# One transformer step on one core: attention with row-half scores, and token-major matmuls of 512 columns

## The chip, the cores and the metric

One core of a Trainium2 chip runs the whole program. The core has TensorE (PE, matmul), VectorE (DVE), ScalarE (ACT), GpSimd (POOL) and SyncE (SP, which here only issues DMAs). TensorE's weight loads have a row of their own in the profile (PEld). Time is device microseconds of one execution; the figure given for a kernel is the median of its runs.

## What is computed

One layer of a diffusion backbone on 640 tokens of width 1024: four tiles of 128 latent tokens and one tile of 128 context tokens. The weight matrices are in float32. Cut to what matters here:

```python
h = rmsnorm(x, norm1_g) * (1.0 + scale1) + shift1          # adaLN, scale and shift from c @ w_ada
q_r, k_r, v_r, g_r, q_d, k_d, v_d, gates = split(h @ w_in)
branch_r = (silu(g_r) * group_norm(retention(q_r, k_r, v_r))) @ w_ret_out
# differential attention, 8 heads, two maps of width 64 in each head:
s = einsum('bqhmd,bkhmd->bhmqk', q_d, k_all) * 64 ** -0.5  # latent queries: 512 latent + 128 cached keys
p = softmax(s, axis=-1)                                    # context queries: 128 context keys
o = einsum('bhqk,bkhe->bqhe', p[:, :, 0] - lam * p[:, :, 1], v_all)
branch_d = (rmsnorm(o, subln_g) * 0.8) @ w_diff_out
x = x + gate1 * ((gate_r * branch_r + gate_d * branch_d) @ w_o)
h2 = rmsnorm(x, norm2_g) * (1.0 + scale2) + shift2
x = x + gate2 * ((silu(h2 @ w_ffn_gate) * (h2 @ w_ffn_up)) @ w_ffn_down)
y = rmsnorm(x, final_norm_g)
```

## The kernel before

Every engine has its own instruction stream, written out by hand, and the streams meet only at semaphores (`wait_ge`, `then_inc`). So the order on each engine is the order in the code.

**Dense phases.** `PHASES` lists 17 of them, in units of 256 columns of a weight matrix. The weights of a unit are a slot of 8 k-tiles x 256 columns; there are two slots. SP streams a unit into `w_raw`, ScalarE rounds it to float32r (`w_hi`, `act_split`), VectorE takes the rest (`w_lo`, `dve_split`), and each product is three matmuls: low x high, high x low, high x high, with the activations split in the same way. Two kinds of unit exist. `pe_T_unit` (line 330) holds weights stationary and streams 320 tokens; its result is feature-major. `pe_N_unit` (line 347) holds 128 tokens stationary and streams 256 weight columns; its result is token-major. The phases v_r, g_r, v_d, w_o, down0, down1 and down2 use the second kind: for each unit, for each of 5 token tiles, for each k, three matmuls. Units of even and odd `par` use PSUM banks 0 to 3 and 4 to 7; `mm_done` is raised after tile 3 and after tile 4 of a unit. The reader takes the four latent tiles in one instruction and the context tile in another (`copy_N` on ScalarE, `residual` on VectorE; `block_sums` then squares on ScalarE). With `split` a phase begins before its input is whole: at the first tile of the first unit TensorE waits at each k.

**Attention.** It works through 8 heads x 5 query tiles, n = 5h + t; tiles 0 to 3 are latent (640 keys), tile 4 is context (128 keys). A tile's stages: GpSimd copies a query tile into `qz`, once for each of two maps, with the other 64 rows at zero; TensorE computes `scores` for a map over all 128 rows (512 + 128 keys) into banks 0 and 1, or 2 and 3; VectorE takes the `maximum`; ScalarE the `exp` with its row sum; VectorE in `weights` the reciprocals, the factor of the second map, and p0 + factor x p1 over all keys; TensorE transposes the result (`weights_T`, banks 4 and 5); ScalarE evacuates it (`evacuate_T`); TensorE multiplies by the values (`outputs`, bank 6 or 7); ScalarE evacuates, in a square with its sum and a scaled copy (`evacuate_o`). The scores of a tile are issued one step ahead of its weights and three ahead of its outputs; the loop runs over heads, the five tiles of a step are written out. All of attention's matmuls are in float32, which the profile shows as two passes each.

After the last transposes GpSimd makes eight products (`diag`, line 635) that TensorE needs to spread the gates over rows.

Of the kernel before, what the change touches and what calls it, by code (L numbers as in the profile page):

```python
# [30 lines left out]
ACT = mybir.ActivationFunctionType  # L31
# [15 lines left out]
DH = 8  # L47
# [20 lines left out]

def lay_out_phases():
# [6 lines left out]
    for name, n, *readers in PHASES:  # L76
        first[name], count[name], reader[name] = unit, n, readers
        before[name] = list(last)
        start[name] = dict(total)
        same = readers[0] == readers[1]  # L80
        for s in range(2):
# [13 lines left out]
PBUF = (0, 1, 2, 0, 1)  # L95
TBUF = (0, 1, 0, 1, 2)
# [20 lines left out]
def tile_of(h, t):  # L117

    return h + t // TILES, t % TILES, h * TILES + t


def build(nc, a, o):

    with ExitStack() as ctx:
# [21 lines left out]
        qz = at("qz", H + 35, [P, TILES, 2, P])  # L146
# [45 lines left out]
        gated = at("gated", M + 10, [P, 4, UC])  # L192
# [26 lines left out]
        sm = small("sm", [P, TILES, 7])  # L219
# [8 lines left out]
        def bank(b, n=BANK, at_=0):  # L228
            return psum[:, b * BANK + at_:b * BANK + at_ + n]

# [11 lines left out]


# [22 lines left out]
        ada_step = sem("ada_step")  # L266

# [16 lines left out]
        at_z, at_qz, at_s, at_max, at_e = sem("at_z"), sem("at_qz"), sem("at_s"), sem("at_max"), sem("at_e")  # L284

        at_r, at_f, at_a, at_T, at_aT, at_o = (sem(n) for n in ("at_r", "at_f", "at_a", "at_T", "at_aT", "at_o"))
        at_oe = sem("at_oe")
# [59 lines left out]
        def pe_N_unit(pe, name, i, par, hi, lo, kt=KT, split=None):  # L347

            for t in range(TILES):
                ts = slice(t * P, (t + 1) * P)  # L350
                for k in range(kt):
                    if split and par == 0 and t == 0:
                        pe.wait_ge(split[0], split[1] + k + 1)
                    for n, (w, x) in enumerate(((w_lo[par], hi), (w_hi[par], lo), (w_hi[par], hi))):
                        last = pe.matmul(bank(4 * par + t // 2, UC, (t % 2) * UC), x[:, k, ts], w[:, k, :],  # L355
                                         start=(k == 0 and n == 0), stop=(k == kt - 1 and n == 2))
                if name in ADA_FIRST and t == LAT_TILES:
                    last = pe_ada_sums(pe, name, i, par)
                if t >= LAT_TILES - 1:
                    last.then_inc(mm_done, 1)  # L360
# [108 lines left out]
        def _(sp):  # L469
# [29 lines left out]

            by_tile = {n: a[n][0].rearrange("(k p) c -> p k c", p=P)  # L500
                       for n in ("w_ret_out", "w_diff_out", "w_o", "w_ffn_gate", "w_ffn_up", "w_ffn_down")}
            stream("v_r", columns(w_in, 1024))
            stream("g_r", columns(w_in, 2048))
# [5 lines left out]
            stream("v_d", columns(w_in, 5120))  # L509
            stream("diff_out", columns(by_tile["w_diff_out"], 0))  # L510
            stream("w_o", columns(by_tile["w_o"], 0))
            for third in range(3):
                c0, kt = third * D, min(KT, FFN // P - third * KT)
                stream(f"up{third}", [(by_tile["w_ffn_gate"], c0, UC, KT), (by_tile["w_ffn_up"], c0, UC, KT)])
                stream(f"down{third}", columns(by_tile["w_ffn_down"][:, third * KT:third * KT + kt, :], 0, kt))
# [11 lines left out]
        def _(pool):  # L527
# [85 lines left out]
            pool.memset(qz[:, :, :, :], 0.0).then_inc(at_z, 1)  # L613
            pool.wait_ge(at_z, 1)

            def fill_qz(t, src):
                for m in range(2):
                    r = slice(m * DHD, (m + 1) * DHD)
                    pool.tensor_copy(qz[r, t, m, :], src(r)).then_inc(at_qz, 1)

            for t in range(TILES):
                fill_qz(t, lambda r: qk_d[r, 0, t * P:(t + 1) * P])
            pool.wait_ge(at_oe, 2)
            pool.dma_start(o["new_diff_k"][0, 0].rearrange("p h m d -> p (h m d)"), k_out[:, :]).then_inc(k_stored, 16)
            with pool.Fori(1, DH) as h:
                for t in range(TILES):
                    pool.wait_ge(at_s, h * (2 * TILES) + (2 * t + 2 - 2 * TILES))
                    fill_qz(t, lambda r: qk_d[r, bass.ds(h, 1), t * P:(t + 1) * P])


            pool.wait_ge(at_T, DH * TILES)
# [12 lines left out]
        def _(pe):  # L644
# [36 lines left out]
            pe_dense(pe, "v_r", pe_N_unit, h_hi, h_lo)  # L681
            pe_dense(pe, "g_r", pe_N_unit, h_hi, h_lo)
# [59 lines left out]
            pe_dense(pe, "v_d", pe_N_unit, h_hi, h_lo)  # L742
# [10 lines left out]
            def scores(h0, t0, m, first=False):  # L753
                h, t, n = tile_of(h0, t0)
                pe.wait_ge(at_qz, n * 2 + (m + 1))
                if not first:
                    pe.wait_ge(at_e, n * 2 + (m - 1))
                if t < LAT_TILES:
                    k = qk_d[:, bass.ds(h + DH, 1), 0:LAT].rearrange("p a i -> p (a i)")
                    pe.matmul(bank(2 * m), qz[:, t, m, :], k, start=True, stop=True)  # L760
                    k = kc_T[:, bass.ds(h, 1), :].rearrange("p a i -> p (a i)")
                    last = pe.matmul(bank(2 * m + 1, P), qz[:, t, m, :], k, start=True, stop=True)  # L762
                else:
                    k = qk_d[:, bass.ds(h + DH, 1), LAT:TOK].rearrange("p a i -> p (a i)")
# [745 lines left out]
```

## Time and profile before

| what | value |
|---|---|
| median of 3 runs | 1433.07 us (1432.6 to 1435.84) |
| profiled execution, span | 1432.7 us |
| TensorE busy | 1363.0 us, 95% |
| weight loads busy | 1291.3 us, 90% |
| VectorE busy | 638.5 us, 45% |
| ScalarE busy | 452.0 us, 32% |
| GpSimd busy | 112.9 us, 8% |
| mean granted TensorE clock | 0.988 of full |

Busy is the time in which at least one instruction of the engine was under way. Matmuls overlap, so 95% does not say that the array works for 95% of the time; how far apart matmuls start says more. Waits of an engine matter where they lie on the chain that ends last.

### The profile page before, as it was taken

To read this page: it belongs to the slowest core of one execution; us is meant where nothing else is said; L and a number is where in the kernel's file an instruction comes from. 1 tells how busy PE (TensorE), PEld (TensorE's weight loads), DVE (VectorE), ACT (ScalarE), POOL (GpSimd) and SP (SyncE) were. 2 spreads that over 40 slices of the span, in tenths; PEclk is the share of its full clock that TensorE was granted. 3 is DMA by queue.
4 is the path that set the end of the run, shared out by engine and by line. 5 is a ranking of instruction groups with operands and counts; after the bars stand their busy time and mean duration, and the time that the engine had idled before them with its cause. 6 is when DMAs were issued, how large, how long until landed. Compare 5 with 4: busy or idle time off the path is not lost.

```text
span 1432.7 us, 24335 instructions
## 1 busy us (share of the span) xinstructions
PE 1363.0 (95%) x9545; PEld 1291.3 (90%) x9545; DVE 638.5 (45%) x935; ACT 452.0 (32%) x777; POOL 112.9 (8%) x205
## 2 busy tenths in 40 slices
PE   4899999999999999998999899989999999999996
PEld 1699998899999999996777599989999999999996
DVE  3733112466557534645777644352324232333244
ACT  5421313344211122216777522242211122212223
POOL 1011000300111111202111300000000000000000
PEclk9999999999999999999999999999999999999998
DMA  9444231143444343530000014202121212221211
GB/s 303 146 116 118 59 88 44 53 134 116 144 150 137 103 128 101 168 128 30 0 0 0 30 59 147 89 30 88 59 88 61 87 59 88 73 75 61 72 45 73
DMA packets 100820, 127.05 MB, mean 89 GB/s; under 512 B 3433, under 2 KB 91986, under 8 KB 100770
## 3 DMA queue, kind: packets, MB, share of 16 engines
q1 hardware_dynamic: 90624, 95.20, 21.1%
q0 software_dynamic: 8928, 30.09, 6.7%
q10 hardware_dynamic: 1218, 1.07, 0.2%
q8 instruction: 34, 0.56, 0.2%
q14 instruction: 16, 0.13, 0.0%
HBM read 115.34 MB, written 4.72 MB: 84 GB/s over the span
## 4 chain that ended last, share of the span: by engine, by line
PE 88%; DVE 4%; issue 2%; SPq 2%; ACT 2%; POOL 1%; DMA 1%; DVEq 0%; ACTq 0%; POOLq 0%
PE psum L340 49%; PE psum L355 26%; PE psum L760 4%; PE psum L787 2%; PE psum L774 2%; SPq L481 1%; PE psum L321 1%; DVE probs L1359 1%; PE psum L762 1%; PE psum L671 1%; DMA ada_a<-in_w_ada 1%; POOL diag L635 1%; PE psum L388 1%; PE psum L389 1%; PE psum L722 1%
## 5 line engine op out<-in xcount | busy, mean ns | idle before, releaser
L305 DVE TENSOR_TENSOR w_lo<-w_raw,w_hi 128x2048 fp32r<-128x2048 f32 x78 | 178.7, 2291 | 307.8 <-ACT w_hi L300 299.8
L340 PE MATMUL psum<-h_hi,w_lo 128*128 128x320 f32 x1344 | 308.5, 311 | 3.4 <-DVE hf L431 1.4
L340 PE MATMUL psum<-h_hi,w_hi 128*128 128x320 f32 x1344 | 307.4, 310 | 0.0
L340 PE MATMUL psum<-h_lo,w_hi 128*128 128x320 f32 x1344 | 307.2, 310 | 0.0
L340 PEld LDWEIGHTS psum<-h_hi,w_lo 128*128 128x128 f32 x1344 | 225.4, 189 | 4.4 <-issue 4.3
L340 PEld LDWEIGHTS psum<-h_lo,w_hi 128*128 128x128 f32 x1344 | 225.9, 189 | 0.0
L340 PEld LDWEIGHTS psum<-h_hi,w_hi 128*128 128x128 f32 x1344 | 225.7, 189 | 0.0
L300 ACT ACTIVATE w_hi<-w_raw 128x2048 fp32r<-128x2048 f32 x77 | 146.8, 1906 | 149.1 <-PE psum L355 97.7
L355 PE MATMUL psum<-w_lo,h_hi 128*128 128x256 f32 x480 | 136.1, 283 | 0.0
L355 PE MATMUL psum<-w_hi,h_lo 128*128 128x256 f32 x480 | 135.8, 283 | 0.0
L355 PE MATMUL psum<-w_hi,h_hi 128*128 128x256 f32 x480 | 135.8, 283 | 0.0
L355 PE MATMUL psum<-w_lo,hid_hi 128*128 128x256 f32 x440 | 124.9, 284 | 1.7 <-DVE hid_lo L1453 1.7
L355 PE MATMUL psum<-w_hi,hid_lo 128*128 128x256 f32 x440 | 124.5, 283 | 0.0
L355 PE MATMUL psum<-w_hi,hid_hi 128*128 128x256 f32 x440 | 124.5, 283 | 0.0
L355 PEld LDWEIGHTS psum<-w_hi,h_lo 128*128 128x128 f32 x480 | 92.1, 192 | 0.0
L355 PEld LDWEIGHTS psum<-w_hi,h_hi 128*128 128x128 f32 x480 | 92.1, 192 | 0.0
L355 PEld LDWEIGHTS psum<-w_lo,h_hi 128*128 128x128 f32 x480 | 92.1, 192 | 0.0
L1140 DVE SCALAR_TENSOR_TENSOR ada_acc<-ada_b,silu_c,ada_acc 128x256 f32<-128x256 f32 x224 | 90.0, 477 | 0.0
L355 PEld LDWEIGHTS psum<-w_lo,hid_hi 128*128 128x128 f32 x440 | 84.4, 192 | 2.6 <-DVE hid_lo L1453 2.6
L355 PEld LDWEIGHTS psum<-w_hi,hid_hi 128*128 128x128 f32 x440 | 84.5, 192 | 0.0
L355 PEld LDWEIGHTS psum<-w_hi,hid_lo 128*128 128x128 f32 x440 | 84.4, 192 | 0.0
L1343 DVE TENSOR_REDUCE sm<-psum 128x1 f32<-128x640 f32 (+1 forms) x80 | 57.4, 717 | 42.5 <-PE psum L762 38.8
(214 smaller groups left out, 1842.6 us busy)
## 6 DMA issues: line engine op xcount, KB each, us to landing
w_raw<-in_w_in SPq DMA_DIRECT2D x32, 1024.0 KB, 5.9
ada_b<-in_w_ada POOLq DMA_DIRECT2D x32, 512.0 KB, 4.1
w_raw<-in_w_ffn_gate SPq DMA_DIRECT2D x11, 1024.0 KB, 5.1
w_raw<-in_w_ffn_up SPq DMA_DIRECT2D x11, 1024.0 KB, 5.1
ada_a<-in_w_ada SPq DMA_DIRECT2D x8, 1024.0 KB, 12.4
w_raw<-in_w_ffn_down SPq DMA_DIRECT2D x8, 1024.0 KB, 5.1
w_raw<-in_w_ret_out SPq DMA_DIRECT2D x4, 1024.0 KB, 5.1
swapped<-qk_d POOLq DMA_DIRECT2D x32, 128.0 KB, 2.5
```

What stands on the lines that cost most here:

```text
L300: act.activation(w_hi[s][:, :, :], w_raw[s][:, :, :], ACT.Copy).then_inc(w_hi_done, 1)
L305: dve.tensor_tensor(w_lo[s][:, :, :], w_raw[s][:, :, :], w_hi[s][:, :, :].bitcast(F32), ALU.subtract).then_inc(w_lo_done, 1)
L321: last = pe.matmul(out[:, 2 * m + c:2 * m + c + 1], ada_acc[:, slot, c, m * P:(m + 1) * P], ones_col[:, :], start=True, stop=True)
L340: last = pe.matmul(bank(4 * par + 2 * j + h, HALF), w[:, k, cs], x[:, k, h * HALF:(h + 1) * HALF], start=(k == 0 and n == 0), stop=(k == K ...
L355: last = pe.matmul(bank(4 * par + t // 2, UC, (t % 2) * UC), x[:, k, ts], w[:, k, :], start=(k == 0 and n == 0), stop=(k == kt - 1 and n = ...
L388: last = pe.matmul(out, x, diagonals[:, t, :], start=True, stop=True) if diagonals is not None else \
L389: pe.transpose(out, x, ident[:, :])
L760: pe.matmul(bank(2 * m), qz[:, t, m, :], k, start=True, stop=True)
L774: last = pe.transpose(bank(4 + c // 4, P, (c % 4) * P), probs[:, PBUF[t], 0, c * P:(c + 1) * P], ident[:, :])
L787: last = pe.matmul(out, aT[:, TBUF[t], c, :], val, start=(c == 0), stop=(c == LAT_TILES or t == LAT_TILES))
L1140: last = dve.scalar_tensor_tensor(acc, w, x, acc, ALU.mult, ALU.add)
L1343: dve.reduce_max(sm[:, t, m:m + 1], psum[:, 2 * m * BANK:2 * m * BANK + size], axis=AX.X, negate=True).then_inc(at_max, 1)
```

## The change

Two things at once.

**Wide phases.** The seven token-major phases work on 512 columns. A unit is now half of the k-tiles x 512 columns, the same bytes in the same slot; two units make a group, and each of 5 token tiles has a bank for its 512 columns (`WIDE_BANKS`, two sets that share banks 6 and 7). Tiles are the outer loop and k the inner one, but in a phase's first unit, where k is outside. A tile is handed on by itself (`wide_done`, `wait_tile`), and readers work tile by tile. The loops over groups are written out.

**Attention.** A map's scores use the 64 rows that hold it, straight from `qk_d`; `qz` is gone. Both maps of a tile lie in three banks (0 to 2 or 3 to 5, by the parity of n), transposes in bank 6 (the fifth one in a free part of the score banks), outputs in bank 7. VectorE takes both maxima in one instruction, combines only the first 128 keys, and evacuates the outputs; GpSimd combines the other 512 keys in two instructions. All 40 tiles are written out, in slots. `sm` has 8 buffers and `probs` 3.

```diff
+WIDE_BANKS = ((0, 1, 2, 6, 7), (3, 4, 5, 6, 7))
-        def pe_N_unit(pe, name, i, par, hi, lo, kt=KT, split=None):
...
+        def pe_wide(pe, name, hi, lo, kt=KT, split=None):
+            r, half = READER[name][0], kt // 2
+            def wait_free(i, t):
+                if i == 0 and t in (0, LAT_TILES - 1):
+                    e, val = BEFORE[name][t // (LAT_TILES - 1)]
+                    pe.wait_ge(freed[e], val)
+                if i == 1 and t >= LAT_TILES - 1:
+                    pe.wait_ge(freed[r], START[name][r] + t + 1)
+                if i == 1 and name in ADA_FIRST and t == 0:
+                    pe.wait_ge(ada_copied, 2)
+            def products(i, par, t, kk):
+                k, ts = par * half + kk, slice(t * P, (t + 1) * P)
+                for n, (w, x) in enumerate(((w_lo[par], hi), (w_hi[par], lo), (w_hi[par], hi))):
+                    last = pe.matmul(bank(WIDE_BANKS[i][t]), x[:, k, ts], wide(w, kk),
+                                     start=(k == 0 and n == 0), stop=(k == kt - 1 and n == 2))
+                return last
+            for i in range(COUNT[name] // 2):
+                for par in range(2):
+                    pe.wait_ge(w_lo_done, unit_of(name, i, par) + 1)
+                    if split and i == 0 and par == 0:
+                        for kk in range(half):
+                            pe.wait_ge(split[0], split[1] + kk + 1)
+                            for t in range(TILES):
+                                if kk == 0:
+                                    wait_free(i, t)
+                                last = products(i, par, t, kk)
+                    else:
+                        for t in range(TILES):
+                            if par == 0:
+                                wait_free(i, t)
+                            for kk in range(half):
+                                if split and i == 0 and t == 0:
+                                    pe.wait_ge(split[0], split[1] + par * half + kk + 1)
+                                last = products(i, par, t, kk)
+                            if par == 1 and t < LAT_TILES:
+                                last.then_inc(wide_done, 1)
+                    if name in ADA_FIRST:
...
+                        last = sums_over_partitions(pe, par, bank(ada_wide_bank(i, par), 4))
+                    last.then_inc(mm_done, 2)
...
+            def stream_wide(name, view, col, kt=KT):
...
+                        sp.wait_ge(w_lo_done, unit_of(name, i, s) - 1)
...
+                        sp.dma_start(w_raw[s][:, 0:2 * half, :].rearrange("p (k h) c -> p k (h c)", h=2),
+                                     view[:, s * half:(s + 1) * half, c:c + WC]).then_inc(w_landed[s], 16)
...
             def copy_N(name, dst, func, after=0):
+                def evacuate(i):
...
+                    for t in range(TILES):
+                        wait_tile(act, name, i, t)
+                        if name in ADA_FIRST and t == LAT_TILES:
+                            copy_ada(name, i, 1, bank(ada_wide_bank(i, 1), 4)).then_inc(ada_copied, 1)
+                        act.activation(dst[:, t, i * WC:(i + 1) * WC], bank(WIDE_BANKS[i][t]), func).then_inc(freed["act"], 1)
...
             def residual(name, g, done0):
+                def evacuate(i):
...
+                        dve.tensor_tensor(gated[:, n % 2, :], bank(WIDE_BANKS[i][t]), gate_row[:, 2 * g + t // LAT_TILES, cs],
+                                          ALU.mult).then_inc(freed["dve"], 1)
...
+                        dve.tensor_tensor(x1[:, t, cs], x1[:, t, cs], gated[:, n % 2, :], ALU.add).then_inc(x1_done, 1)
...
-            pool.memset(qz[:, :, :, :], 0.0).then_inc(at_z, 1)
...
-                    pool.tensor_copy(qz[r, t, m, :], src(r)).then_inc(at_qz, 1)
...
+            pool.wait_ge(k_copied, 1)
             pool.dma_start(o["new_diff_k"][0, 0].rearrange("p h m d -> p (h m d)"), k_out[:, :]).then_inc(k_stored, 16)
...
+            for n in range(QT):
...
+                pool.wait_ge(at_f, n + 1)
+                pool.tensor_scalar(p1, p1, sm[:, n % 8, 6:7], None, ALU.mult).then_inc(at_w, 1)
+                pool.wait_ge(at_w, n + 1)
+                pool.tensor_tensor(p0, p0, p1, ALU.add).then_inc(at_a, 1)
...
+            def scores(n):
...
+                if n >= 2:
+                    pe.wait_ge(at_e, 2 * n - 2)
+                if n >= 4:
+                    pe.wait_ge(at_aT, n - 3)
+                m0, m1 = slice(0, DHD), slice(DHD, P)
...
                 if t < LAT_TILES:
+                    pe.matmul(bank(b0 + 1, P), qk_d[m0, h, q], kc_T[m0, h, :], start=True, stop=True).then_inc(at_shared, 1)
+                    pe.matmul(bank(b0 + 2, LAT - P), qk_d[m1, h, q], qk_d[m1, k, P:LAT], start=True, stop=True)
+                    pe.matmul(bank(b0), qk_d[m0, h, q], qk_d[m0, k, 0:LAT], start=True, stop=True)
+                    pe.matmul(bank(b0 + 2, P, LAT - P), qk_d[m1, h, q], kc_T[m1, h, :], start=True, stop=True)
+                    pe.wait_ge(at_shared, n - h + 1)
+                    last = pe.matmul(bank(b0 + 1, P, LAT - P), qk_d[m1, h, q], qk_d[m1, k, 0:P], start=True, stop=True)
                 else:
+                    pe.matmul(bank(b0, P), qk_d[m0, h, q], qk_d[m0, k, LAT:TOK], start=True, stop=True)
+                    last = pe.matmul(bank(b0 + 2, P), qk_d[m1, h, q], qk_d[m1, k, LAT:TOK], start=True, stop=True)
                 last.then_inc(at_s, 1)
+            def weights_T(n):
+                full = keys_of(n) == TOK
+                if full:
+                    pe.wait_ge(at_av, n - n // TILES + 1)
+                if n >= 1:
+                    pe.wait_ge(at_aT, n)
+                for c in range(keys_of(n) // P):
+                    if c == (DVE_KEYS // P if full else 0):
+                        pe.wait_ge(at_a, n + 1)
+                    if c == LAT_TILES and n + 2 < QT:
+                        pe.wait_ge(at_e, 2 * (n + 2) + 2)
+                    out = last_keys_T(n) if c == LAT_TILES else bank(6, P, c * P)
+                    last = pe.transpose(out, probs[:, n % 3, 0, c * P:(c + 1) * P], ident[:, :])
+                last.then_inc(at_T, 1)
...
+            pe.wait_ge(k_copied, 1)
+            for slot in range(-1, QT + 4):
+                if 0 <= slot - 3 < QT:
+                    weights_T(slot - 3)
+                if 0 <= slot - 4:
+                    outputs(slot - 4)
+                if slot + 1 < QT:
+                    scores(slot + 1)
...
+            for slot in range(QT + 3):
+                if slot >= 3:
+                    evacuate_T(slot - 3)
+                if slot < QT:
+                    exp(slot)
...
+            def maximum(n):
+                dve.wait_ge(at_s, n + 1)
...
+                dve.reduce_max(sm[:, n % 8, 0:2], both, axis=AX.X, negate=True).then_inc(at_max, 1)
+            def factor(n):
...
+                if keys_of(n) == TOK:
+                    p0, p1 = probs[:, n % 3, 0, 0:DVE_KEYS], probs[:, n % 3, 1, 0:DVE_KEYS]
+                    dve.wait_ge(at_f, n + 1)
+                    dve.scalar_tensor_tensor(p0, p1, v[:, 6:7], p0, ALU.mult, ALU.add).then_inc(at_av, 1)
+            def evacuate_o(n):
...
+                dve.wait_ge(at_o, n + 1)
+                dve.tensor_scalar(out, x, r0, None, ALU.mult).then_inc(at_oc, 1)
+                dve.wait_ge(at_oc, n + 1)
+                dve.scalar_tensor_tensor(junk_o[:, :], x, r0, out, ALU.mult, ALU.mult,
+                                         accum_out=stats[:, n:n + 1]).then_inc(at_oe, 1)
+            for slot in range(-1, QT + 4):
+                if 0 <= slot - 1 < QT:
+                    factor(slot - 1)
+                if 0 <= slot - 4:
+                    evacuate_o(slot - 4)
+                if slot + 1 < QT:
+                    maximum(slot + 1)
```

## Rows read from the trace of the kernel before

**Rows 1.** The page, part 4: the chain that ended last, by line.

```profile
PE psum L340 49%; PE psum L355 26%; PE psum L760 4%; PE psum L787 2%; PE psum L774 2%; SPq L481 1%; PE psum L321 1%; DVE probs L1359 1%; PE psum L762 1%; PE psum L671 1%; DMA ada_a<-in_w_ada 1%; POOL diag L635 1%; PE psum L388 1%; PE psum L389 1%; PE psum L722 1%
```

**Rows 2.** The same chain in order of time: start us, us, what.

```profile
117.78 115.21 PE psum L355 x960
...
474.36 112.74 PE psum L340 x768
...
667.33 0.77 PE psum L774 x5
...
771.52 0.77 PE psum L774 x5
```

**Rows 3.** Groups by form, TensorE: busy us, mean ns; idle before, its end.

```profile
L355 PE MATMUL psum<-w_lo,hid_hi 128*128 128x256 f32 x440 | 124.9, 284 | 1.7 <-DVE hid_lo L1453 1.7
...
L355 PE MATMUL psum<-w_lo,mix_hi 128*128 128x256 f32 x160 | 45.5, 284 | 1.1 <-DVE mix_lo L1406 1.1
```

**Rows 4.** Timeline inside attention: start us, us, engine, what, idle before it.

```profile
743.64 0.27 PE L774 MATMUL psum<-ident,probs 128*128 128x128 f32 x1
...
743.75 1.02 PE L760 MATMUL psum<-qk_d,qz 128*128 x2
...
743.84 0.82 DVE L1343 TENSOR_REDUCE sm<-psum 128x1 f32<-128x640 f32 x1 [1.11 <-PE psum L762]
...
744.70 0.79 ACT L1031 ACTIVATE probs<-psum,sm 128x640 f32<-128x640 f32 x1 [0.70 <-DVE sm L1343]
...
744.83 1.06 PE L787 MATMUL psum<-v_d,aT 128*128 x8
...
745.94 1.02 PE L760 MATMUL psum<-qk_d,qz 128*128 x2
```

**Rows 5.** Timeline at the end of w_o.

```profile
930.19 0.28 PE L355 MATMUL psum<-w_hi,mix_hi 128*128 128x256 f32 x1
...
930.70 0.42 DVE L1423 TENSOR_TENSOR gated<-psum,gate_row 128x256 f32<-128x256 f32 x1 [0.18 <-DVE x L1425]
...
933.93 0.17 DVE L1147 TENSOR_REDUCE stats<-stats 128x5 f32<-128x20 f32 x1 [2.24 <-ACT junk L868]
```

**Rows 6.** Groups by form, VectorE, ScalarE and GpSimd (DVE, ACT, POOL).

```profile
L1343 DVE TENSOR_REDUCE sm<-psum 128x1 f32<-128x640 f32 x64 | 52.8, 824 | 39.0 <-PE psum L762 38.8
...
L1031 ACT ACTIVATE probs<-psum,sm 128x640 f32<-128x640 f32 x64 | 50.8, 794 | 31.9 <-DVE sm L1343 28.9
...
L1038 ACT ACTIVATE aT<-psum 128x640 f32<-128x640 f32 x32 | 22.4, 699 | 0.0
...
L635 POOL TENSOR_TENSOR diag<-ident,mod 128x512 f32<-128x512 f32 x8 | 12.0, 1527 | 0.1
...
L1356 DVE TENSOR_SCALAR sm<-sm,lamv 128x1 f32<-128x1 f32 x40 | 10.9, 273 | 1.5
...
L1354 DVE RECIPROCAL sm<-sm 128x2 f32<-128x2 f32 x40 | 6.3, 157 | 0.0
...
L1343 DVE TENSOR_REDUCE sm<-psum 128x1 f32<-128x128 f32 x16 | 4.6, 287 | 3.6 <-PE psum L765 3.6
...
L579 POOL COPY state<-s_ends 128x256 f32<-128x256 f32 x8 | 3.0, 403 | 0.0
...
L1359 DVE SCALAR_TENSOR_TENSOR probs<-probs,sm 128x128 f32<-128x128 f32 x8 | 2.8, 344 | 0.0
```

**Rows 7.** Timeline: attention's first scores and its last transpose.

```profile
651.30 1.19 PE L760 MATMUL psum<-qk_d,qz 128*128 128x512 f32 x1 [1.38 <-POOL qz L619]
...
793.93 0.30 PE L774 MATMUL psum<-ident,probs 128*128 128x128 f32 x1 [1.06 <-ACT aT L1038]
```

**Rows 8.** Stretches: us, busy of each engine (instructions), clock, DMA share, GB/s.

```profile
150.00:230.00 80.00, 80.00 (x669) 80.00 (x668) 12.84 (x6) 17.65 (x17) 0.00 (x0) 1.00 0.27 79
216.00:288.00 72.00, 67.36 (x406) 59.67 (x405) 25.84 (x72) 26.41 (x47) 14.44 (x20) 1.00 0.18 54
648.00:654.00 6.00, 3.94 (x15) 2.52 (x15) 0.59 (x3) 3.00 (x5) 4.34 (x11) 0.74 0.22 87
```

More of the change, by code:

```diff
@@ L66, with wide_ready @@
           ("down1", 4, "dve", "dve"), ("up2", 6, "act", "dve"), ("down2", 4, "dve", "dve")]
+WIDE = ("v_r", "g_r", "v_d", "w_o", "down0", "down1", "down2")
+WC = 2 * UC
+WIDE_BANKS = ((0, 1, 2, 6, 7), (3, 4, 5, 6, 7))
+def wide_ready(name, i, t):
+    return (2 * WIDE.index(name) + i) * LAT_TILES + t + 1
 def lay_out_phases():
@@ L80, in lay_out_phases @@
         same = readers[0] == readers[1]
+        if name in WIDE:
+            total[readers[0]] += TILES * (n // 2)
+            last = [(readers[0], total[readers[0]] - 4), (readers[0], total[readers[0]])]
+            unit += n
+            continue
         for s in range(2):
@@ L345, in pe_T_unit, with wide @@
                 last.then_inc(mm_done, 1)
-        def pe_N_unit(pe, name, i, par, hi, lo, kt=KT, split=None):
[L349 to L360, printed above, removed]
+        def wide(w, k):
+            return w[:, 2 * k:2 * k + 2, :].rearrange("p a b -> p (a b)")
@@ L508, in _ @@
             stream("k_d", columns(w_in, 4096))
-            stream("v_d", columns(w_in, 5120))
+            stream_wide("v_d", w_in, 5120)
             stream("diff_out", columns(by_tile["w_diff_out"], 0))
-            stream("w_o", columns(by_tile["w_o"], 0))
+            stream_wide("w_o", by_tile["w_o"], 0)
             for third in range(3):
@@ L775, in weights_T, with outputs @@
                 last.then_inc(at_T, 1)
-            def outputs(h0, t0):
-                h, t, n = tile_of(h0, t0)
+            def outputs(n):
+                h, t = n // TILES, n % TILES
                 pe.wait_ge(at_aT, n + 1)
-                pe.wait_ge(at_oe, n + (2 if t == 0 else 1))
-                out = bank(6 + t % 2, P)
-                for c in range(TILES if t < LAT_TILES else 1):
-                    if t == LAT_TILES:
-                        val = v_d[:, LAT_TILES, bass.ds(h * P, P)]
-                    else:
-                        val = v_d[:, c, bass.ds(h * P, P)] if c < LAT_TILES else v_cache[:, bass.ds(h * P, P)]
-                    last = pe.matmul(out, aT[:, TBUF[t], c, :], val, start=(c == 0),
-                                     stop=(c == LAT_TILES or t == LAT_TILES))
-                last.then_inc(at_o, 1)
@@ L815, in _ @@
-            pe.wait_ge(at_oe, 2 + DH * TILES)
+                if n >= 1:
+                    pe.wait_ge(at_oe, n)
+                hs = slice(h * P, (h + 1) * P)
+                chunks = keys_of(n) // P
+                for c in range(chunks):
+                    val = v_d[:, LAT_TILES, hs] if t == LAT_TILES else v_d[:, c, hs] if c < LAT_TILES else v_cache[:, hs]
+                    last = pe.matmul(bank(7, P), aT[:, n % 3, c, :], val, start=(c == 0), stop=(c == chunks - 1))
+                last.then_inc(at_o, 1)
@@ L832, in _ @@
                 kt = COUNT[f"up{third}"]
-                pe_dense(pe, f"down{third}", pe_N_unit, hid_hi, hid_lo, kt=kt, split=(hid_l, tiles + AHEAD))
+                pe_wide(pe, f"down{third}", hid_hi, hid_lo, kt=kt, split=(hid_l, tiles + AHEAD))
                 tiles += kt
@@ L1091, in _ @@
             set_table(ACT.Sqrt)
[L1092 removed]
+            dense_wide("w_o", block_sums("norm2", "w_o", 0))
             root("norm2", TILES)
@@ L1266, in rotate @@
                 return evacuate
-            nothing = lambda i, par: None
+            nothing = lambda i: None
             dve.wait_ge(ld_rope, 16)
             dense("qk_r", rotate("qk_r", qk_r, 0, 0, 2, 0))
-            dense("v_r", nothing)
-            dense("g_r", nothing)
+            dense_wide("v_r", nothing)
+            dense_wide("g_r", nothing)
             with dve.Fori(0, RH) as h:
@@ L1330, in _ @@
             dense("k_d", rotate("k_d", qk_d, 8, DH, 4, 128 + 256))
-            dense("v_d", nothing, peel=1)
+            dense_wide("v_d", nothing)
             dve.wait_ge(freed["act"], START["diff_out"]["act"])
```

351 lines of the change are left out of this document (133 added, 218 removed).

## The prediction

> **What bounds the kernel now.** I read four views in this order. The chain of work that ended last comes first: it runs mostly through TensorE, at line 340 (`pe_T_unit`, 320 columns per matmul) and line 355 (`pe_N_unit`, 256 columns) [rows 1], all of its large entries TensorE's. So a dense phase is worth what its matmul stream is worth. The "ns of one" of a matmul is no price, since matmuls overlap; the chain's long stretches give the cadence [rows 2]: 115.21 us / 960 = 120.0 ns at 256 columns, 112.74 / 768 = 146.8 ns at 320. Next I read the chain inside attention: the same transposes come back six heads later after 771.52 - 667.33 = 104.19 us, 17.37 us per head [rows 2]. There TensorE's queue is nearly full: four latent tiles and one context tile need 16.1 us of it (below), so attention is bound by TensorE, with about 1 us per head lost to waits. The timeline and the groups by form then give durations, and the windows the granted clock.
>
> **Wide phases (v_r, g_r, v_d, w_o, down0 to down2).** Six phases of 480 matmuls and one of 360, 3240 in all, become 1620 of 512 columns; the arithmetic stays. From the two cadences [rows 2]: (146.8 - 120.0)/64 = 0.419 ns per column, and 120.0 - 256 x 0.419 = 12.8 ns per matmul. At 512 columns that is 227.2 ns against 2 x 120.0, so 12.8 ns x 1620 = **-20.8 us**. Before has no 512-column matmul of this kind. Bounds: cost proportional to columns (240 ns), no gain; no fixed cost left (214.4 ns), -41.5. I take the fixed cost as fixed, because it comes from two rows of this very stream.
>
> By the Trainium skill (TensorE: Matmul & The Clock Gate, the section on packing small matmuls) a weight load overlaps a running matmul only if it goes to another row group. Then half the loads gone would give 1620 x 0.11 us (the pace of small fp32 passes in rows 4) = 178 us. The trace speaks against it: 120.0 ns has no room for load and matmul in series.
>
> The tile-outermost order moves the waits. Before, the first unit of a phase needs all k of its input within its first tile, and TensorE waits 1.7 us in the down phases and 1.1 in w_o [rows 3]. After, the first unit takes only the first half of k, 60 x 0.227 = 13.6 us of work, and the late half is ready by then: **-2.8 us**; nothing is late next. The end of a phase: from the last matmul of w_o (930.19 + 0.28) to the total on VectorE (933.93) pass 3.5 us, since the four latent tiles were evacuated as one piece and ScalarE runs five squares behind it [rows 5]. After, only the last tile is open: multiply and add of 128x512 at 0.69 each (0.42 at 256 wide, and 1.05 ns for each element more), a square of some 0.8 (the 640-wide copy takes 0.70 [rows 6]) and handoffs: 2.4 us. **-1.1** in w_o, and again in down2. Given back, **+0.8** in all: the last tile of g_r and v_d is 512 wide instead of 256, some 0.2 each, and in v_d TensorE's group 1 stands behind ScalarE's copy of unit 1's sums, an estimate of 0.4 for a small operation and its handoffs. The 28 weight DMAs keep their bytes, in runs twice as long, and SP's waits are the same. ScalarE's and VectorE's splits lie beside the stream, busy 17.7 and 12.8 us of 80 [rows 8]; with VectorE's 1.4 us per tile against 2.7 between tiles they stay hidden, and would show only if the stream ran 2.6 times faster (80 / (17.7 + 12.8)). This half: -20.8 - 2.8 - 2.2 + 0.8 = **-25.0 us**.
>
> **Attention, TensorE** [rows 4]. Before, one latent score map takes 743.75 to 744.83 = 1.08 us, two 2.17; ten output passes take 744.83 to 745.94 = 1.11; a transpose 0.11, five 0.55. That is 3.83 per latent tile, 0.78 per context tile, 16.1 per head. After, each map has its own half of the array's rows, with no zeros. If the halves run side by side, in order, each fp32 product being two passes of 0.11 (128 keys), 0.32 (384) or 0.43 (512), the second map's 384 keys follow from 0.11 on beside the first map's, and all end at 1.30 us. One after another it is 2.17. Before shows no half-row matmul; the bounds are 1.08 and 2.17. I take 1.30, because neighbouring matmuls in the queue then share neither rows nor bank. Per head: 4 x (0.55 + 1.11 + 1.30) + 0.66 = 12.5 us. Each slot changes twice between full and half rows. Unlike full-row matmuls follow each other at 0.11; at most the change costs the rest of one small matmul's own time, 0.27 - 0.11 = 0.16. I take 0.05, nearer to the cadence: 13.0 per head.
>
> The Trainium skill (TensorEngine Tiling (Array Packing), Key Properties) says that changing the tiling mode drains the engine. That rule speaks against this change; no row of before shows such a change of mode.
>
> **The other engines** [rows 6]. VectorE per latent tile: one maximum over 1280 elements at 1.05 ns each, 1.49; reciprocal, factor and a 128-key combination, 0.86 with gaps; two output operations taken from ScalarE, at the combination's 0.34: 3.0, and 1.6 for a context tile, 13.6 per head. ScalarE: two exponentials of 0.79 and the copies, 2.5. GpSimd loses the 80 copies into qz and gets two operations over 512 keys: the sum at 1.53, the product between 0.40 (a copy of half the size) and 1.53: 2.0 to 3.1 per latent tile. It is read two slots later, so its length is covered up to a slot's; beyond, weights_T would wait for it.
>
> The round that sets the slot: the fifth transpose waits for the exponentials two tiles ahead (0.11), outputs 1.11, scores 1.30 + 0.10 and 0.16 to their end, maximum 1.49, two exponentials 1.58, four handoffs of 0.05 (744.66 to 744.70 in rows 4): 6.05 us for two slots, 15.1 per head. Laying out the instructions of all 40 slots in their queues' order with these durations also gives 15.1; before's order, laid out the same way, gives 17.4, and the trace has 17.37. So 8 x 15.1 = 120.8, and 5.0 to fill (before 142.9 - 138.9 = 4.0; the transposes now stand a slot later): 125.8 against 142.9 from the first scores to the last transpose, 651.30 to 794.2 [rows 7]. VectorE's new wait for outputs, ahead of the next maximum, is in that order. The first scores now wait for k_out's copy in place of qz, which I put at nothing. What follows stays: GpSimd's eight products of 1.53 start after the last transpose. **Attention -17.1 us.**
>
> **Sum.** -25.0 - 17.1 = -42.1. The profiled execution has a span of 1432.7, the runs a median of 1433.07: 1432.7 - 42.1 = 1390.6, as a run about **1391 us**.
>
> **Rivals.**
> 1. The forecast, 1391, its own range 1384 to 1402: chance 0.54.
> 2. Each change of array mode costs the full 0.16: the round is 6.3, 15.7 per head, +5: 1396. For it nothing in the trace; against it that unlike matmuls follow at cadence. 0.14. It is the tiling page's rule in the Trainium skill, priced from rows.
> 3. The row halves don't run side by side; the change does not do what it says. TensorE needs 16.6 per head, the slots in order 18.3: attention +8.5 instead of -17.1: 1417, from 1411 to 1424. For it: nothing in before shows two matmuls sharing the array. 0.20.
> 4. A 512-column matmul costs two of 256: 1412. Against it the two cadences. 0.04.
> 5. The other side: TensorE's clock falls in attention to its lower level (1.2 of 2.4 GHz). It was granted 0.74 from 648 to 654, where one-column sums, eight transposes and gaps came before the first scores; with fewer columns to stream this could recur. TensorE's 104 us would double: it decides from 40% of the stretch (42.1/104); all of it gives about 1495. Against it: the retention stage kept 1.00 with 406 matmuls in 72 us [rows 8]. 0.05.
> 6. Case 3 with the full price of 2 (19.2 per head, 1424) and half of 4: 1434, no change. 0.03.
>
> **The numbers.** The likeliest case gives 1391. Cases 1, 2 and 4 and half of 3 lie between 1384 and 1419, about 8 in 10; what is left out is the slow end of case 3, cases 5 and 6, and a low tail. 0.2% (2.9 us) is about what a measurement of this kernel can tell from no change. Faster: 0.54 + 0.14 + 0.20 + 0.04 = 0.92; within 0.2%: 0.03; slower: 0.05.
>
> **What the profile after would show.** Dense phases: 512-column matmuls 227 ns apart, v_r and g_r unbroken in 109 us (before 115.2); 240 ns makes case 4 right. Attention: a head every 15.1 us; in the score line, the second map's matmuls starting before the first map's are through, 1.3 us from first to last. 2.2 us means case 3; gaps at the changes between scores and the rest mean case 2. No idle TensorE on hid_lo or mix_lo; about 2.4 us from w_o's last matmul to the total. GpSimd at 2.0 to 3.1 us per latent tile; if weights_T waits for it, that term is wrong. The prediction fails if the halves are serial, if VectorE's queue needs more than 15 us per head, or if windows of attention show a clock of 0.5.

## The result, and the profile after

The changed kernel takes 1394.74 us (median of 4 runs, 1391.44 to 1399.02), the kernel before in the same session 1433.87; the ratio is 0.973, with an interval of 0.9705 to 0.9754. The prediction said 1391 us, from 1384 to 1419. The runs spread with the granted clock: 1391.44 us at a mean of 0.990, 1399.02 at 0.980. The profiled execution has a span of 1393.5 us, 39.2 less than before (1432.7).

The chain that ended last in the changed kernel, in order of time (start us, us, what); line 396 is the wide matmul, 367 `pe_T_unit`, 879 `outputs`, 707 and 709 GpSimd's two instructions, 332 VectorE's split:

```profile
119.21 108.84 PE psum L396 x480
...
467.59 112.74 PE psum L367 x768
...
672.21 1.13 PE psum L879 x10
...
687.34 1.12 PE psum L879 x10
...
747.87 2.13 PE psum L879 x10
...
757.02 1.73 POOL probs L707
758.82 1.26 POOL probs L709
760.12 1.73 POOL probs L707
...
791.81 56.57 PE psum L367 x384
...
851.44 10.02 DMA x<-in_x_prompt
861.48 2.30 DVE w_lo L332
863.83 41.13 PE psum L396 x180
904.99 0.70 DVE gated L1467
```

Set against [rows 2], the 960 matmuls of 120.0 ns became 480 of 226.75 ns (108.84 / 480); a 320-column phase is as before, 112.74. A head takes 687.34 - 672.21 = 15.13 us instead of 17.37. New are a wait of w_o for a DMA, and GpSimd on the chain at the end of attention.

The first and last matmuls of attention, by the timeline of the changed kernel:

```profile
641.96 0.55 PE L844 MATMUL psum<-kc_T,qk_d 64*128 64x128 f32 x1 [1.26 <-ACT k_out L1100]
...
770.80 0.27 PE L867 MATMUL psum<-ident,probs 128*128 128x128 f32 x1
```

In the kernel before, the matmuls of diff_out begin on the chain at 814.75 us, in the changed kernel at 791.81 (above):

```profile
814.75 56.57 PE psum L340 x384
```

With these the stages come out as follows (us; before from the chain of the kernel before and [rows 7]).

| stage | before | after | difference | predicted |
|---|---|---|---|---|
| v_r and g_r | 115.2 | 108.8 | -6.4 | -6.1 |
| v_d, first to last unit | 61.1 | 58.5 | -2.5 | -2.5 |
| attention, first scores to last transpose | 142.6 | 128.8 | -13.8 | -17.1 |
| from there to diff_out | 20.8 | 21.0 | +0.2 | 0 |
| diff_out to the end | 617.9 | 601.7 | -16.2 | -16.5 |

What is left of the 39.2, -0.5 us, lies in stages that the change does not touch.

Groups by form of the changed kernel (busy us, mean ns of one, idle before and its end), to be held against [rows 3, 6]:

```profile
L396 PE MATMUL psum<-w_lo,hid_hi 128*128 128x512 f32 x220 | 85.6, 389 | 0.0
...
L707 POOL TENSOR_SCALAR probs<-probs,sm 128x512 f32<-128x512 f32 x32 | 52.7, 1648 | 19.3 <-DVE sm L1407 19.1
...
L1400 DVE TENSOR_REDUCE sm<-psum 128x2 f32<-128x1280 f32 x32 | 47.7, 1490 | 15.3 <-PE psum L849 15.2
...
L709 POOL TENSOR_TENSOR probs<-probs 128x512 f32<-128x512 f32 x32 | 41.3, 1291 | 2.7
...
L396 PE MATMUL psum<-w_lo,mix_hi 128*128 128x512 f32 x80 | 31.3, 391 | 1.8 <-DVE w_lo L332 1.8
```

The idle time on hid_lo and mix_lo is gone, as predicted; in w_o a wait for w_lo has come in its place. And one latent slot, PE's part of the timeline: outputs, the scores of both maps (first map 844 and 846, second 845, 847 and 849), transposes:

```profile
703.21 0.39 PE L879 MATMUL psum<-v_cache,aT 128*128 128x128 f32 x2
703.53 0.37 PE L844 MATMUL psum<-kc_T,qk_d 64*128 64x128 f32 x1
703.53 0.59 PE L845 MATMUL psum<-qk_d 64*128 64x384 f32 x1
...
703.85 0.59 PE L846 MATMUL psum<-qk_d 64*128 64x512 f32 x1
703.96 0.48 PE L845 MATMUL psum<-qk_d 64*128 64x384 f32 x1
...
704.50 0.38 PE L849 MATMUL psum<-qk_d 64*128 64x128 f32 x2
704.82 0.55 PE L867 MATMUL psum<-ident,probs 128*128 128x128 f32 x3
```

The second map's 384 keys start at the same time as the first map's 128. From the first score to the last one's second pass (704.50 + 0.11) pass 1.08 us and 0.11 more to stream it: 1.19, where [rows 4] have 2.17.

### The profile page after: what moved, and what is told of

Same layout as the page of the kernel before. It is cut to its first block, busy times and chain, and to the rows that moved or that the text cites. A ratio compares the mean times of both kernels' runs of the same rounds, so it can differ in the third digit from the quotient of the medians.

```text
span 1393.5 us, 20140 instructions
## 1 busy us (share of the span) xinstructions
PE 1318.9 (95%) x7989; PEld 1203.3 (86%) x7989; DVE 643.9 (46%) x1023; ACT 424.9 (30%) x655; POOL 185.1 (13%) x204
## 3 DMA queue, kind: packets, MB, share of 16 engines
q1 hardware_dynamic: 76800, 95.20, 21.5%
## 4 chain that ended last, share of the span: by engine, by line
PE 86%; DVE 5%; ACT 3%; issue 2%; DMA 2%; POOL 1%; DVEq 0%; SPq 0%; ACTq 0%
PE psum L367 50%; PE psum L396 25%; PE psum L879 2%; ACT probs L1109 1%; PE psum L348 1%; PE psum L867 1%; DMA x_nat<-in_x_prompt 1%; DVE ada_acc L1195 1%; DVE sm L1400 1%; PE psum L846 1%; PE psum L464 1%; DMA x<-in_x_prompt 1%; PE psum L465 1%; PE psum L802 1%; DVE o_nat L1438 1%
## 5 line engine op out<-in xcount | busy, mean ns | idle before, releaser
L396 PE MATMUL psum<-w_lo,h_hi 128*128 128x512 f32 x240 | 93.7, 390 | 0.4 <-ACT mod L1007 0.4
L396 PE MATMUL psum<-w_hi,h_hi 128*128 128x512 f32 x240 | 93.4, 389 | 0.0
L396 PE MATMUL psum<-w_hi,h_lo 128*128 128x512 f32 x240 | 93.4, 389 | 0.0
L396 PE MATMUL psum<-w_hi,hid_lo 128*128 128x512 f32 x220 | 85.6, 389 | 0.0
L396 PE MATMUL psum<-w_lo,hid_hi 128*128 128x512 f32 x220 | 85.6, 389 | 0.0
L396 PE MATMUL psum<-w_hi,hid_hi 128*128 128x512 f32 x220 | 85.6, 389 | 0.0
L707 POOL TENSOR_SCALAR probs<-probs,sm 128x512 f32<-128x512 f32 (+1 forms) x40 | 57.6, 1439 | 22.2 <-DVE sm L1407 22.0
L1109 ACT ACTIVATE probs<-psum,sm 128x640 f32<-128x640 f32 (+1 forms) x80 | 56.0, 708 | 13.6 <-DVE sm L1400 11.6
L1400 DVE TENSOR_REDUCE sm<-psum 128x2 f32<-128x1280 f32 (+1 forms) x40 | 51.0, 1276 | 15.3 <-PE psum L849 15.2
L396 PEld LDWEIGHTS psum<-w_hi,h_hi 128*128 128x128 f32 x240 | 45.0, 188 | 9.5
```

The lines of the kernel that those rows point to most:

```text
L396: last = pe.matmul(bank(WIDE_BANKS[i][t]), x[:, k, ts], wide(w, kk), start=(k == 0 and n == 0), stop=(k == kt - 1 and n == 2))
L707: pool.tensor_scalar(p1, p1, sm[:, n % 8, 6:7], None, ALU.mult).then_inc(at_w, 1)
L1109: act.activation(probs[:, n % 3, m, 0:size], scores_at(n, m), ACT.Exp, bias=sm[:, n % 8, m:m + 1], accum_out=sm[:, n % 8, 2 + m:3 + m]).th ...
L1400: dve.reduce_max(sm[:, n % 8, 0:2], both, axis=AX.X, negate=True).then_inc(at_max, 1)
```

## The experiments

**One half at a time.** Two kernels take one half of the change each; the phases and streams of the other half are those of before.

```diff
# wide_alone, against before (and the same for the six other phases)
-            pe_dense(pe, "v_r", pe_N_unit, h_hi, h_lo)
+            pe_wide(pe, "v_r", h_hi, h_lo)
# attention_alone, against the changed kernel (and the same for the six others)
-            pe_wide(pe, "v_r", h_hi, h_lo)
+            pe_dense(pe, "v_r", pe_N_unit, h_hi, h_lo)
```

> The kernel before with the seven wide phases only; attention as before. The prediction's half sum is -25.0 us. Read from the stages of the two traces: v_r and g_r 108.84 instead of 115.21 us, v_d 2.5 us shorter, and from the start of diff_out to the end 16.3 us less, -25.2 in all. So 1433.9 - 25 = about 1409 us, with TensorE waiting once for VectorE's split of w_o's second unit as in the changed kernel (1.8 us). Rival: the two halves only pay together (the phases around attention overlap with it), then under 20 us are gained, 1414 or more.

> The kernel before with the new attention only; the token-major phases on 256 columns. The prediction's term is -17.1 us: 1417. The trace of the changed kernel shows 149.9 us from the first scores to diff_out against 163.4 before, -13.5, of which the spells of half clock in attention (two more than before) may be some 2 to 3 us: by this reading 1418 to 1421. Where it comes out at 1417, the missing 3 us of the combination lie in the clock or in a meeting of the two halves; at 1420 they belong to attention itself.

Measured beside 1435.7 us for the kernel before: wide phases alone 1407.73 us, ratio 0.9792 (0.9775 to 0.9809); attention alone 1418.71 us, ratio 0.9885 (0.9868 to 0.9901). Each half pays by itself, -28.0 and -17.0 us by the medians; the rival for the wide half is out. Their sum is 45 against 39 for both, more than the traces bear out: attention from first scores to diff_out takes 149.7 us alone and 149.8 in the combination, and v_r and g_r take 108.84 us with or without the new attention. By the traces, 4.0 us of the difference stand ahead of attention, in code that attention_alone shares with the kernel before: its first scores come at 647.29 us instead of 651.30, and up to there the trace of before has four spells at the lower clock, that of attention_alone none. Another 1.3 us stand in w_o, where TensorE waits 0.5 us for w_lo in wide_alone and 1.8 in the combination. The median of attention_alone, 1418.7, lies between the two values (1417 and 1420) that were to tell where the missing 3 us of attention are; its trace, with 149.7 us, puts them in attention itself. One spell at the lower clock in attention_alone (707.0 to 710.4 us) reads so on its chain, the output passes of two tiles that follow each other:

```profile
706.94 1.97 PE psum L803 x10
...
711.66 1.12 PE psum L803 x10
```

They stand 4.7 us apart instead of 3.1: 1.6 us for one spell. Such spells differ from run to run in number and place, so the last 2 to 3 us of any sum here aren't settled by medians.

**The two halves of the array.**

```diff
# same_rows
-                m0, m1 = slice(0, DHD), slice(DHD, P)
+                m0, m1 = slice(0, DHD), slice(0, DHD)
# map_by_map: the five products of a latent tile in the order
#   before: first map 128, second 384, first 512, second 128, second 128
#   now:    first map 128, first 512, second 384, second 128, second 128
```

> The changed kernel, but the second map's scores are computed from rows 0 to 63 as well, so that both maps of a tile use the same half of the array (the second map is then a copy of the first; sizes, order, banks and waits stay). Theory: the halves run side by side because they lie in different rows. Then the latent scores grow from 1.20 to about 2.17 us, every latent slot from 3.10 to about 4.1, a head from 15.13 to 18.3 to 19.2 us, and the time to 1394.7 + 8 x 3.2 to 4.1 = 1420 to 1428. Rival: the scores got shorter for another reason (no zeros to stream, three banks, the order of the five products); then the head stays at 15.1 and the time within 3 us of 1394.7.

Measured: 1428.0 us, at the upper end of what was expected, with 19.25 us per head in the middle of attention and a spell of 20.5 us at the lower clock at its start. The scores, one after another on the same rows:

```profile
706.42 0.48 PE L844 MATMUL psum<-kc_T,qk_d 64*128 64x128 f32 x2
706.74 0.81 PE L845 MATMUL psum<-qk_d 64*128 64x384 f32 x2
707.39 1.02 PE L846 MATMUL psum<-qk_d 64*128 64x512 f32 x2
...
708.47 0.38 PE L849 MATMUL psum<-qk_d 64*128 64x128 f32 x2
```

From 706.42 to the end of the last one's second pass (708.69) are 2.27 us against 1.19. With shared rows the gain of attention is lost, and more (wide_alone, with the old attention, took 1407.73 us in the same session): the different rows carry it, not the missing zeros, the banks or the order.

> The changed kernel with the five score products of a latent tile in another order: first both products of the first map (128 and 512 keys), then the three of the second (384, 128, 128); in the changed kernel the two maps alternate. Theory: TensorE takes its queue in order, so a product over rows 64 to 127 can run beside one over rows 0 to 63 only where it stands next to it. Then the second map begins with the first map's last pass: first to last start of the scores grows from 1.09 to about 1.7 us, a latent slot from 3.10 to about 3.75, a head from 15.13 to 17.4 to 17.7, the time to 1413 to 1416. Rival: the queue is not held by order where the rows differ; then the two maps still run beside each other and the time stays within 3 us of 1394.7.

Measured: 1393.59 us; my theory of the order is wrong. The same slot there:

```profile
707.29 0.37 PE L844 MATMUL psum<-kc_T,qk_d 64*128 64x128 f32 x1
707.30 0.59 PE L846 MATMUL psum<-qk_d 64*128 64x384 f32 x1
...
707.61 0.59 PE L845 MATMUL psum<-qk_d 64*128 64x512 f32 x1
707.73 0.48 PE L846 MATMUL psum<-qk_d 64*128 64x384 f32 x1
```

The second map's first product (line 846 there) stands third in the code and starts 0.01 us after the first one, ahead of the 512 keys that stand before it. Matmuls on different rows did not wait for each other's turn in the code. Whether the engine put them so, or the compiler had already changed their order, the record does not show.

**The price of changing between full and half rows.**

```diff
# extra_half: in outputs(n), ahead of its products; extra_full has slice(0, P)
+                if t < LAT_TILES:
+                    rows = slice(0, DHD)
+                    pe.matmul(bank(7, P, P), qk_d[rows, h, 0:P], ident[rows, :], start=True, stop=True)
```

> The changed kernel with one more product of 128 columns over 64 rows between the transposes and the outputs of each latent tile (written to a free part of bank 7, never read): two more changes between full and half rows per latent slot. Theory: a change costs 0.09 us into half rows and 0.09 + 0.055 back, as the gaps of 0.205 and 0.202 + 0.165 against 0.112 and 0.11 in the changed kernel show. Then a latent slot grows from 3.10 by 0.22 for the product and 0.24 to 0.34 for the changes, to about 3.56 to 3.66 us. Rival: the gaps there belong to the semaphore waits at these places; then the slot grows like that of the twin run with full rows, to 3.32.

> The twin of the run before: the same extra product over all 128 rows, so no extra change of mode. Both theories: a latent slot grows by two passes of 0.11, from 3.10 to 3.32 us.

Measured, one run each: 1409.37 and 1396.74 us. Transposes, extra product (line 877), outputs and the next scores, first with half rows, then with full rows:

```profile
711.66 0.76 PE L867 MATMUL psum<-ident,probs 128*128 128x128 f32 x5
712.36 0.48 PE L877 MATMUL psum<-ident,qk_d 64*128 64x128 f32 x2
712.77 1.16 PE L882 MATMUL psum<-v_d,aT 128*128 128x128 f32 x8
...
714.08 0.37 PE L844 MATMUL psum<-kc_T,qk_d 64*128 64x128 f32 x1
```

```profile
708.47 0.77 PE L867 MATMUL psum<-ident,probs 128*128 128x128 f32 x5
709.07 0.39 PE L877 MATMUL psum<-ident,qk_d 128*128 128x128 f32 x2
709.30 1.06 PE L882 MATMUL psum<-v_d,aT 128*128 128x128 f32 x8
...
710.51 0.37 PE L844 MATMUL psum<-kc_T,qk_d 64*128 64x128 f32 x1
```

From the transposes to the next scores pass 2.42 and 2.04 us: a pair of changes costs 0.38 us, 0.19 each, a little more than the 0.24 to 0.34 that the gaps had suggested. From outputs to outputs a latent slot takes 3.71 us with the extra half-row product and 3.33 with the full-row one; the waits are the same in both kernels, so the rival of the waits falls. The price is near rival 2's (0.16), not the 0.05 of the forecast. The Trainium skill (TensorEngine Tiling (Array Packing), Key Properties) says that a change of tiling mode drains the engine; the trace agrees as far as a cost goes, 0.38 us for the way there and back.

**What sets the pace, and a faster order.**

```diff
# context_last, against the changed kernel; the places that use these, and the two counts that number latent tiles, follow
+def place(n):
+    return (n // LAT_TILES, n % LAT_TILES) if n < DH * LAT_TILES else (n - DH * LAT_TILES, LAT_TILES)
-    return TOK if n % TILES < LAT_TILES else P
+    return TOK if n < DH * LAT_TILES else P
```

> The changed kernel with the 8 context tiles of attention worked at its end, after all 32 latent tiles, instead of one in each head. Theory, read from the trace after: a latent slot is 3.10 us and TensorE's queue in it has no gap, so TensorE sets it; what is left of a head, 15.13 - 4 x 3.10 = 2.73 us, is one short slot with 1.7 us in which TensorE waits for the loop of maximum and exponentials. Packed together, the short slots go at the pace of VectorE's queue, some 1.7 us: 8 x (2.73 - 1.7) = -8 us, and 1 to 2 us less at the end, where GpSimd no longer paces the last latent tiles: 1385 to 1387. Rival 1, the prediction's own account (a round of 6.05 us for any two slots): the order of tiles changes nothing, 1394. Rival 2: GpSimd (2.94 us per latent tile) or VectorE (3.0) needs the context tile to catch up; then latent slots become longer than 3.2 us and the time is 1398 or more.

Measured: 1383.67 us, ratio 0.9634 (0.9616 to 0.9652). Its chain in the latent slots is TensorE without a break; transposes of one slot, outputs, transposes of the next, outputs (the scores stand between them):

```profile
695.01 0.69 PE psum L872 x5
695.71 1.12 PE psum L884 x10
...
698.12 0.69 PE psum L872 x5
698.81 1.12 PE psum L884 x10
```

From 658 to 739 us every latent slot is 3.10 us. Both rivals fall: the order of tiles matters, and GpSimd and VectorE keep up without the context tile. So TensorE sets a latent slot, and the loop through maximum and exponentials costs time only beside a context tile.

The time came out a little below the expected 1385 to 1387. The context tiles at the end followed each other at 1.46 us, not 1.7, while the clock stood at its upper level. From 754.4 us it was at its lower level for 13.7 us, and they followed each other at 1.77. In both_edits (below) it fell at 758.1 us, and the step from 1.46 to 1.77 us came later too. The lower clock cost some 0.3 us for each tile there; whether the packing brought it on is not shown. The stretch in context_last (us, busy time of PE, PEld, DVE, ACT and POOL, granted clock, DMA):

```profile
755.00:767.00 12.00, 7.72 (x23) 4.58 (x22) 7.04 (x27) 3.92 (x15) 9.38 (x13) 0.50 0.00 1
```

**The new wait in w_o.**

```diff
# both_edits, on top of context_last
-            dve.wait_ge(ld_x1, 32)
             dense_wide("w_o", residual("w_o", 0, 0))
# and in residual's evacuate, ahead of the first tile
+                    if name == "w_o" and i == 0:
+                        dve.wait_ge(ld_x1, 32)
```

> The kernel with the context tiles last, and VectorE's wait for the reload of x1 moved from ahead of w_o's weight splits to the first residual, which is the first to use x1. Theory: in the changed kernel w_o's second split stands behind that wait (reload landed at 861.48 us, split until 863.8) and TensorE has 1.8 us of idle time on w_lo; x1 itself is needed only when w_o's first group is done, some 14 us later. So TensorE's idle time on w_lo in w_o goes and the time falls by 1.8 us from 1383.7 to 1381.9. Rival: the reload lands late enough, or the split starts late for another reason (ScalarE's w_hi), that the idle time only changes its name: 1383.7.

Measured: 1381.69 us (1379.37 to 1387.38), ratio 0.9649 (0.9629 to 0.967). The intervals of the two kernels overlap, so the times do not show the step; the groups by form do, first of context_last, then of this kernel:

```profile
L401 PE MATMUL psum<-w_lo,mix_hi 128*128 128x512 f32 x80 | 32.0, 400 | 1.9 <-DVE w_lo L337 1.9
```

```profile
L401 PE MATMUL psum<-w_lo,mix_hi 128*128 128x512 f32 x80 | 31.1, 389 | 0.0
```

From its first matmul to its last, w_o takes 54.2 us here, 56.4 in the changed kernel, and 58.0 in context_last, where a spell at the lower clock begins at 853.4 us, in w_o. By the median this kernel is the fastest of the study, about 13 us under the changed one; by the ratios to the kernel before (0.9649 and 0.9634) it can't be told from context_last.

**The clock at the start of attention.**

```diff
# fill_start: at the head of each slot's work on TensorE
+                for c in range(10 if slot < 3 else 5 if slot == 3 else 0):
+                    pe.matmul(bank(7, P, P), qk_d[:, 0, 0:P], ident[:, :], start=True, stop=True)
```

> The changed kernel with 45 more full-row products of 128 keys, written to a free part of bank 7 and never read, in the first five slots of attention, where TensorE waits for the first exponentials (no transposes or outputs exist yet). Question: whether the spells of half clock at the start of attention (642.0 to 645.4 and 655.6 to 659.0 us in the changed kernel's trace) follow the gaps in TensorE's work there. Theory: they do; with the gaps filled the granted clock stays at 1.00 from 645 to 665, the first ten outputs come up to 1.6 us per spell earlier, less the work added where it is not hidden: 1392 to 1395. Rival: the spells come whatever TensorE does there; then the clock shows them still, and the added work costs 0 to 3 us: 1395 to 1398.

Measured: 1398.96 us (1394.56 to 1401.48), above both expected ranges; the profiled run is the fastest of the four. Stretches of the changed kernel and of this one (us, busy time of PE, PEld, DVE, ACT and POOL, granted clock, DMA):

```profile
640.00:645.00 5.00, 3.74 (x22) 3.22 (x22) 0.59 (x2) 2.51 (x3) 0.94 (x2) 0.70 0.52 210
...
655.00:660.00 5.00, 4.86 (x26) 4.21 (x27) 1.96 (x7) 1.55 (x7) 4.83 (x4) 0.66 0.02 3
```

```profile
640.00:645.00 5.00, 4.54 (x37) 4.19 (x38) 0.72 (x1) 1.80 (x3) 0.53 (x1) 1.00 0.41 165
...
655.00:660.00 5.00, 3.67 (x31) 2.98 (x29) 2.96 (x7) 2.32 (x6) 4.19 (x4) 1.00 0.00 0
```

In the profiled run the clock stays at its upper level (2.4 GHz) where it had fallen to the lower one (1.2), as the theory has it. But nothing is won: attention takes 149.8 us again, so what the clock gave back, the added products cost, and by the medians the kernel is slower if anything. The other runs had mean clocks of 0.985 to 0.987 against 0.991, so spells came in them here or elsewhere. What brings a spell on is not settled.

## Why the prediction was right, and where it was not

- **Wide phases.** Right to 1 us: 226.75 ns against 227.2, so 1620 x (240.0 - 226.75) = -21.5 against -20.8. The fixed cost per matmul is real. A gain of 178 us from halved weight loads, which the Trainium skill's rule on weight loads (TensorE: Matmul & The Clock Gate, the packing section) would have meant as the prediction priced it, is nowhere in the trace.
- **The moved waits.** hid_lo and mix_lo 0.0, as said. From w_o's last matmul to the total 907.19 - 904.96 = 2.2 us (2.4 said). The 0.4 estimated for v_d's copy of the sums is the 0.4 us that the groups show on line 396. The step that failed is "nothing is late next": VectorE waits for the reload of x1 ahead of w_o's splits. Before, the wait lay there too, hidden with little to spare: the second unit's split was done at 885.36 us, and TensorE came to that unit at 887.11, 15.96 us after w_o's first matmul. In the changed kernel TensorE comes to it 13.6 us after the first matmul, since the first unit is shorter and the waits on mix_lo within it are gone, and the reload took 10.0 us from its issue instead of 8.5. The split was done too late and TensorE waited 1.8 us, more than the 1.1 saved on mix_lo. In wide_alone, with a reload of 8.75 us, it waited 0.5. Why the reload took longer is not shown.
- **The row halves.** Right in mechanism (same_rows), 1.19 us against 1.30. The reason given, that neighbours in the queue share neither rows nor bank, was half of it: the rows decide, and the products need not be neighbours in the code (map_by_map).
- **Changes of mode.** Mis-sized: 0.34 to 0.38 us per slot against 0.10, some 1.2 to 1.4 us per head; 0.19 for one change is also above the 0.16 taken as its upper bound. TensorE needs not 13.0 us per head but 13.4: 15.13 less the 1.7 that it waits, in three gaps around the context tile (0.6, 0.3 and 0.8 us). That it is only 0.4 more comes from the scores: by the prediction's own pass times the two halves side by side need 1.08 us and not 1.30, and 0.10 of the price of the changes stands within the measured 1.19.
- **The head.** 15.13 against 15.1, but by compensation, and so in part by luck. The forecast took a round of 6.05 us through maximum and exponentials for any two slots. In truth a latent slot is bound by TensorE (3.10 instead of 3.03, the mode changes in it), and the slot around a context tile is shorter, 15.13 - 4 x 3.10 = 2.73. context_last shows the difference: by the round of 6.05 us it would have changed nothing. How the layout of all 40 slots, which gave 15.1 too, had the single slots is not on record. With the price of a change near rival 2's, the total of 1394.7 also lies nearer to rival 2's 1396 than to 1391, but the head did not grow to the 15.7 of that rival.
- **GpSimd.** 1.65 + 1.29 = 2.94 us, inside 2.0 to 3.1, the first one above the 1.53 taken as its upper bound. Covered in the middle; the last head's four latent tiles are paced by it (757.02, then 760.12 on the chain).
- **Attention's sum.** -13.8 to the last transpose instead of -17.1. Of the missing 3 us, 1.6 are a spell of half clock in the seventh head: its outputs begin at 747.71 us and the eighth's at 764.44, 16.73 us apart instead of 15.13. map_by_map, whose trace has no spell there, takes 127.5 us for the stage instead of 128.8. The rest lies in the fill and the end, GpSimd's pace and two more spells among them; their shares are open. Rival 5 was thus true in small: three spells of 3.4 us in this stretch, where before had one.
- **What follows attention** cost the same 21 us, as said, but not in the same way: GpSimd's products took 10.0 instead of 12.0 us, and VectorE's scaling of the outputs, 7.5 us, became the last to end.

## What to carry to other kernels

When a phase is re-tiled, look for every wait that stands on another engine ahead of that phase's work: a first unit that is over sooner needs its next operand sooner, and a wait that was hidden with little to spare comes out. Work that uses half of the array's rows pays when its twin uses the other half, less about 0.4 us for each time that the queue goes there and back. A period that comes out as forecast is no proof of what sets it; move the short item elsewhere and see whether the period holds.

## What the hardware showed unasked

Matmuls on different row halves started without regard to their order in the code (0.01 us apart in map_by_map), whether by the engine or by the compiler. And VectorE can stand behind GpSimd: in the kernel with the context tiles last, a 128x128 combination that takes 0.35 us elsewhere took 1.40, to 0.15 us after the end of a GpSimd instruction that began 0.02 us sooner:

```profile
742.27 1.27 POOL L714 TENSOR_TENSOR probs<-probs 128x512 f32<-128x512 f32 x1
742.29 1.40 DVE L1416 SCALAR_TENSOR_TENSOR probs<-probs,sm 128x128 f32<-128x128 f32 x1
```

By the Trainium skill (SBUF — State Buffer, the section on its two sides) an operation of VectorE with two SBUF inputs and one of GpSimd that reads SBUF exclude each other for a whole instruction; these rows agree in that VectorE's ends only after GpSimd's. In the changed kernel the same form has a mean of 435 ns, where it took 344 before [rows 6]:

```profile
L1411 DVE SCALAR_TENSOR_TENSOR probs<-probs,sm 128x128 f32<-128x128 f32 x32 | 13.9, 435 | 1.1
```

Of these 32, 22 took 0.35 us; the ten longer ones (eight of 0.45, one of 1.11 and one of 1.45) each ended 0.15 us after the end of a GpSimd instruction that ran beside them.
